# Router matmuls turned round, and three rounds of five expert places in the first expert loop

## The reference, cut to what matters

```python
def routed_moe(h2d, router_w, router_b, w_gate, w_up, w_down):
    aff = jax.nn.sigmoid(jnp.dot(h2d, router_w).astype(F32))      # tokens x 16
    ...  # best group of four experts, the best two experts in it, weights wts
    def expert_block(args):
        xblk, e = args
        hid = jax.nn.silu(xblk @ w_gate[e]) * (xblk @ w_up[e])    # 1024 -> 1024
        return hid @ w_down[e]
    ...
    out = jnp.zeros((n_tok + 1, d_), F32).at[row_tok].add(yb * row_w[:, None])
```

## Time and profile before

| | us |
|---|---|
| median of 3 runs (2302.38 to 2303.32) | 2302.49 |
| the profiled execution, its own time | 2303.21 |
| its span in the trace | 2301.4 |
| PE busy in the span | 2105.7 (91%) |
| layer 0, end of the shift to first expert matmul | 524.6 to 562.5 |
| layer 0, expert places | 562.5 to 1090.9 |
| layer 1, end of the shift to first expert matmul | 1307.2 to 1329.9 |

### The profile page before, as it was taken

One profiled execution on the slowest core, in us unless ns is written; L12 is line 12 of the kernel. 1 busy time (PEld: TensorE's weight loads), 2 busy tenths in 40 slices (PEclk: granted clock), 3 DMA queues, 4 the chain that ended last, 5 costly groups with the idle time before them and its releaser, 6 DMA issues.

```text
span 2301.4 us, 26458 instructions
## 1 busy us (share of the span) xinstructions
PE 2105.7 (91%) x10534; PEld 1152.9 (50%) x10534; DVE 692.6 (30%) x1682; ACT 403.2 (18%) x862; POOL 48.0 (2%) x64
## 2 busy tenths in 40 slices
PE   5999999897999999999499799999999899998997
PEld 2345447745333333444275733333333676577886
DVE  2045118524111111110438311111111588711411
ACT  2014210012111111000216211111111332421101
POOL 0000000001000000000100000000000000000000
PEclk8999999996999999999699899999999899798998
DMA  9661229111999999998330279999999633232240
GB/s 361 234 220 37 73 89 389 51 69 57 400 427 429 427 428 427 428 427 312 132 110 2 98 330 428 429 428 428 428 429 422 237 109 100 94 127 102 80 140 19
DMA packets 114049, 572.94 MB, mean 249 GB/s; under 512 B 6080, under 2 KB 20672, under 8 KB 89264
## 3 DMA queue, kind: packets, MB, share of 16 engines
q1 hardware_dynamic: 105568, 545.57, 59.2%
q0 software_dynamic: 5648, 20.47, 2.4%
q10 hardware_dynamic: 2752, 5.77, 0.6%
HBM read 562.87 MB, written 8.91 MB: 248 GB/s over the span
## 4 chain that ended last, share of the span: by engine, by line
PE 77%; DMA 13%; DVE 6%; ACT 2%; issue 2%; SPq 1%; PEld 0%; POOL 0%; ACTq 0%; DVEq 0%; PEldq 0%; POOLq 0%
PE banks L494 25%; DMA weight_ring<-in_moe_w_down 7%; PE banks L925 6%; PE banks L876 6%; PE banks L1024 4%; PE banks L910 4%; PE banks L508 3%; DMA weight_ring<-in_moe_w_up 3%; PE banks L706 2%; PE banks L979 2%; PE banks L892 2%; PE banks L1011 2%; PE banks L686 2%; PE banks L537 2%; DVE pages L1789 1%
## 5 line engine op out<-in xcount | busy, mean ns | idle before, releaser
L494 PE MATMUL banks<-pages,weight_ring 128*128 128x256 f32 (+1 forms) x2240 | 578.9, 419 | 11.2 <-DVEq L2312 3.4
L494 PEld LDWEIGHTS banks<-pages,weight_ring 128*128 128x128 f32 x2240 | 428.9, 193 | 160.1 <-issue 106.5
L925 PE MATMUL banks<-weight_ring,pages 128*64 128x512 f32 x1024 | 228.5, 597 | 5.9 <-DMA weight_ring<-in_moe_w_up 5.9
L1581 ACT ACTIVATE pages<-banks 128x512 f32<-128x512 f32 (+1 forms) x149 | 82.2, 572 | 676.3 <-PE banks L1024 129.0
L1472 ACT ACTIVATE pages<-banks 128x256 f32<-128x256 f32 (+2 forms) x214 | 92.0, 452 | 603.8 <-PE banks L494 426.5
L876 PE MATMUL banks<-weight_ring,pages 128*64 128x512 f32 x832 | 185.6, 601 | 8.5 <-DMA weight_ring<-in_moe_w_up 3.8
L1789 DVE TENSOR_TENSOR pages<-banks,pages 128x512 f32<-128x512 f32 (+3 forms) x157 | 90.3, 616 | 294.4 <-PE banks L1037 147.4
L1789 DVE TENSOR_TENSOR pages<-pages 128x512 f32<-128x512 f32 (+9 forms) x271 | 163.6, 628 | 8.3 <-DVE pages L1789 2.5
L1789 DVE TENSOR_TENSOR pages<-pages,banks 128x512 f32<-128x512 f32 (+1 forms) x41 | 28.2, 687 | 455.2 <-PE banks L925 219.8
L925 PEld LDWEIGHTS banks<-weight_ring,pages 128*64 128x64 f32 x1024 | 71.4, 137 | 157.9 <-issue 141.4
L1024 PE MATMUL banks<-weight_ring,pages 128*64 128x512 f32 x512 | 114.9, 597 | 13.1 <-DVE pages L2214 12.5
(11 more groups left out here) (281 smaller groups left out, 1877.4 us busy)
## 6 DMA issues: line engine op xcount, KB each, us to landing
weight_ring<-in_moe_w_gate SPq DMA_DIRECT2D x64, 2048.0 KB, 17.9
weight_ring<-in_moe_w_up SPq DMA_DIRECT2D x64, 2048.0 KB, 21.1
weight_ring<-in_moe_w_down SPq DMA_DIRECT2D x64, 2048.0 KB, 20.5
weight_ring<-in_ada_w SPq DMA_DIRECT2D x24, 2048.0 KB, 16.2
weight_ring<-in_even_w_in SPq DMA_DIRECT2D x18, 2048.0 KB, 19.8
weight_ring<-in_odd_w_in SPq DMA_DIRECT2D x8, 2048.0 KB, 8.8
weight_ring<-in_odd_w_out SPq DMA_DIRECT2D x6, 2048.0 KB, 8.1
weight_ring<-in_odd_w_qkv SPq DMA_DIRECT2D x3, 2048.0 KB, 10.6
```

What stands on the lines that cost most here:

```text
L494: last = pe.matmul(b[:, 0:w], s[:, k, m * P:(m + 1) * P], src(k)[:, t0:t0 + w], start=(k == 0), stop=(k == nk - 1))
L925: last = pe.matmul(b[64 * a:64 * a + 64], xg[:, par, k, 64 * half:64 * half + 64], w_[:, k, 512 * a:512 * a + 512], start=(half == 0 and k ...
L1581: act.activation(dst, banks_mem[:, use(l, job)[0], 0:n], func).then_inc(moe_taken(l, job, 0)[0], 1)
```

## The change

Router: the stationary side is now the 16 router columns of a channel block and the 16 columns behind them (32 in all), on the column group `k % 4`; the moving side is `H[:, k]` with all tokens (512 or 256). Each of the 8 matmuls waits only for its own block of `H`. Four partial sums, 32 rows each, come out in `router_part`, which ACT copies to `pages`; a matmul with `fold` as the moving side for each tile of tokens adds the four and gives tokens x 16 as before. It stands behind the first 8 transposes.

First expert loop: the order of the places is now middle, narrow, middle, narrow, wide, three times, and a narrow one. There are as many of each kind as before. The loop holds five places and runs three times. `par` and `1 - par` are replaced by the table `BUFFER`; a wide place and the middle place behind it both use buffer 0. The layer 1 loop is what it was.

```diff
-KINDS = [MIDDLE, NARROW] * 6 + [WIDE, NARROW, WIDE, WIDE]
+FIVE = [MIDDLE, NARROW, MIDDLE, NARROW, WIDE]
+KINDS = FIVE * 3 + [NARROW]
...
+    router_part = pages(8, 512)
...
+    BUFFER = (0, 1, 0, 1, 0, 0)
...
-            pe.wait_ge(sem("norm_h"), norm_before(f"norm_e{l}") + KT * (nt // 2))
-            job = ("router", l)
+            job = ("router_part", l)
             b = open_job(job)
-            rw = vec("router_w").rearrange("p (k e) -> p k e", k=KT)
-            for t in range(nt):
-                for k in range(KT):
-                    last = pe.matmul(b[:, t * 16:(t + 1) * 16], H[:, k, t * P:(t + 1) * P], rw[:, k],
-                                     start=(k == 0), stop=(k == KT - 1))
+            at = VEC["router_w"][0]
+            for k in range(KT):
+                j = k % 4
+                pe.wait_ge(sem("norm_h"), norm_before(f"norm_e{l}") + (k + 1) * (nt // 2))
+                last = pe.matmul(b[32 * j:32 * j + 32, 0:w], small[:, at + 16 * k:at + 16 * k + 32], H[:, k, 0:w],
+                                 start=(k < 4), stop=(k >= 4), tile_position=(0, 32 * j))
             close_job(job, last)
...
+                if t == 0:
+                    wait_taken(pe, ("router_part", l))
+                    job = ("router", l)
+                    b = open_job(job)
+                    for t2 in range(nt):
+                        last = pe.matmul(b[:, 16 * t2:16 * t2 + 16], router_part[:, t2 * P:(t2 + 1) * P],
+                                         S("fold", 0, 16), start=True, stop=True)
                     close_job(job, last)
...
-                with pe.Fori(0, LOOPED[l], 2) as e:
-                    expert(p, e, 0, KINDS[0])
-                    expert(p, e + 1, 1, KINDS[1])
-                for e in range(LOOPED[l], N_EXP):
-                    expert(p, e, e % 2, KINDS[e])
+                if l == 0:
+                    with pe.Fori(0, 3) as i:
+                        for c in range(5):
+                            expert(p, i * 5 + c, BUFFER[c], FIVE[c], BUFFER[c + 1])
+                    expert(p, 15, BUFFER[5], NARROW, BUFFER[0])
+                else:
+                    with pe.Fori(0, N_EXP, 2) as e:
+                        expert(p, e, 0, NARROW, 1)
+                        expert(p, e + 1, 1, NARROW, 0)
...
             shift(f"norm_e{l}", l, 1, w)
+            evac(("router_part", l), router_part[:, 0:w], w)
             b = result(act, ("router", l))
...
-                gather(g + 1, 1 - par)
+                gather(g + 1, then)
```

More of the change, by code:

```diff
@@ L773, in experts @@
                         last = pe.transpose(b[:, k * P:(k + 1) * P], H[:, 4 * half + k, t * P:(t + 1) * P], ident)
+                    close_job(job, last)
+                if t == 0:
[5 more added lines that the diff above has]
+                                         S("fold", 0, 16), start=True, stop=True)
                     close_job(job, last)
@@ L848, in gather, with expert @@
                     turn_picked(g)
-            def expert(p, e, par, kind):
+            def expert(p, e, par, kind, then):
                 it = g = p * N_EXP + e
@@ L1590, in gather, with expert @@
                     take("spread", g, spread[:, par].rearrange("p n m -> p (n m)"), n=2 * P)
-            def expert(p, e, par, kind, rows_out=None):
+            def expert(p, e, par, kind, then, rows_out=None):
                 it = g = p * N_EXP + e
@@ L1644, in experts @@
             with act.Fori(0, np_) as p:
[L1645 to L1650, removed]
+                if l == 0:
+                    with act.Fori(0, 3) as i:
+                        for c in range(5):
+                            row = i * FIVE_ROWS + sum(FIVE[:c])
+                            expert(p, i * 5 + c, BUFFER[c], FIVE[c], BUFFER[c + 1], y_dram[bass.ds(row, FIVE[c])])
+                    expert(p, 15, BUFFER[5], NARROW, BUFFER[0], y_dram[ROWS_AT[15]:ROWS_AT[15] + NARROW])
+                else:
+                    with act.Fori(0, N_EXP, 2) as e:
+                        expert(p, e, 0, NARROW, 1)
+                        expert(p, e + 1, 1, NARROW, 0)
                 if l == 0:
@@ L2179, in add_rest, with expert @@
                 tt(y_rest[:, 512:1024], rest[32:64], hid[32:64, 1], ALU.add).then_inc(moe_taken(0, "dn1", 0)[0], 1)
-            def expert(p, e, par, kind, after=None):
+            def expert(p, e, kind, rest=None):
                 it = g = p * N_EXP + e
@@ L2190, in expert @@
                 select_slots(g + 1, col)
-                if l == 0 and after == MIDDLE:
-                    add_rest(it - 1, p * KINDS.count(MIDDLE) + e // 2 + 1)
+                if rest is not None:
+                    add_rest(it - 1, rest)
                 if l == 0:
@@ L2236, in experts @@
                     dve.sem_inc(sem("rows_known"), 1)
[L2237 to L2241, removed]
+                if l == 0:
+                    with dve.Fori(0, 3) as i:
+                        for c in range(5):
+                            expert(p, i * 5 + c, FIVE[c], 6 * p + 2 * i + (c + 1) // 2 if c in (1, 3) else None)
+                    expert(p, 15, NARROW)
+                else:
+                    with dve.Fori(0, N_EXP, 2) as e:
+                        expert(p, e, NARROW)
+                        expert(p, e + 1, NARROW)
                 if l == 0:
```

3 lines of the change are left out of this document (1 added, 2 removed).

## The result

The changed kernel takes 2285.24 us in the median of 4 runs (2278.15 to 2287.58), the kernel before, beside it, 2302.90. The ratio is 0.9917, with a 95% interval of 0.9895 to 0.9940: faster by 0.8%. The forecast was 2283.5, in a range of 2279 to 2290.5. The profiled execution took 2287.58 and has a span of 2285.5, 15.9 less than before.

The account below looks back on a forecast made before the run. PE bounds the kernel, through router work everybody awaits and waits for weights in layer 0's expert places. Terms 8.6 - 1.5 + 9.0 + 3.5 - 0.7 = 18.9 us gave a median of 2283.5, range 2279 to 2290.5.

Parts of the forecast that it names:

- The router in layer 0: Layer 0, end of ACT's shift to sigmoid: sigmoid at 529.85 instead of 538.50, 8.6 us earlier, at the lower clock.
- the end named for that case: Layer 0 router at full clock: transposes and fold halve, ACT's table load is late next, gain 10.8 us.
- The clock behind it: Layer 0 ranking up to 1.8 us slower, first middle place up to 2.4 more; 1.5 us charged of 0 to 4.2.
- Layer 1: Layer 1 router: sigmoid at 1310.8 instead of 1314.31, 3.5 us gained, less 0.7 charged for the clock.
- the 9.0 of starving: Layer 0 expert places: PE's time lost to late weight chunks, 9.0 us, all regained by the new order.
- The state behind a wide place: Layer 0 expert loop: weight ring full again after each wide place (PE 44.3 us, transfers 31.5), so later rounds don't starve.
- The end of the places: Behind layer 0's last place: smaller store against about 5 us of queued transfers; put at 0, between gain 2.3 and loss 3.
- the first rival: Layer 0 expert loop fetched again, two turns at 3 to 5 us plus clock dips: 6 to 10 us lost; 7%.
- the full price of 12 us: Second rival: loop fetch costs 12 us at each turn plus 2.4 of lower clock, 28.8 us, giving 2312; 4%.
- The starving didn't move: Third rival, layer 0 places: transfers don't catch up under the wide place; at most half of 9.0 gained, 2288 to 2292.5; 9%.
- the ends of the forecast: Whole kernel: 2279 with 10.8 in router, no clock price, smaller store; 2288 with 7.5 in places, full clock price, half the queue.
- The fourth rival: Routers of both layers: something else ends last, so their 10.9 us are lost, giving 2294.4; 4%.

Follow-up runs that it names:

- the experiment with the wide place last: Changed kernel with the odd_w_out chunks held until the y_rows gathers landed, plus the third wide place moved from place 14 to the end: 2277.67 us.
- the loop of eight: Changed kernel with the layer 1 expert loop made eight places a turn instead of two: 2286.40 us, in a single run.

## Why the prediction was right, point by point

- **The median** was forecast at 2283.5 and came out at 2285.24; the gain was 17.7 us by the medians and 15.9 in the profiles, for 18.9.
- **The router in layer 0**: 8.6 us forecast to the sigmoid, 10.9 measured. The step that failed is the clock of the stretch: I had left PE at the lower one, and its work under the shift brought back the full one from 523.6. It is the end named for that case, 10.8. ACT's copy and table load were then late next, as written there.
- **The clock behind it**: the ranking took 1.9 us more, just beyond what was allowed (1.8), while the first place, charged with up to 2.4 more, took 0.7 less. To the first place the gain is 37.94 - 29.08 = 8.9 us. With the 0.7 in the first place it is 9.6, for the 7.1 forecast with both charges.
- **Layer 1**: 4.3 to the sigmoid for 3.5, and 3.3 to the first expert matmul for 2.8. Where the clock rose to the full level, the rest followed the same steps.
- **The places**: 9.5 us in the profile of both changes together, 0.7 of it from the clock. That leaves 8.7 (9.46 - 0.74) for the 9.0 of starving; no wait for weights is left. The state behind a wide place is as it was reckoned, and the experiment with the wide place last starved by 5.1 us where the same arithmetic said 6.
- **The end of the places**: this is the term that was wrong. It was put at 0, between -3 and +2.3, and cost 4.4 us, beyond its end. The step that failed is "about 5 us of transfers are still queued": the queue was seen, but its price was taken from the store alone, and not from the eight gathers behind it, in front of which three chunks of 2 MB were issued. The store gained more than the 2.3 allowed, 4.0 us, but up to DVE's first sum the gathers lost 3.3 and in its wait for the second pair 4.1; the other 1.0 lies in small pieces. The 29.35 us of the kernel before already held 7.5 us of delay by the same chunks.
- **The sum was right in part since two misses cancel**: 2.5 more in layer 0's router and 0.5 in layer 1's, 4.4 less at the end; another 1.2 in the profile lie ahead of the router (0.85) and in the rest (0.4), where no work was changed.
- **The rivals**: in the changed kernel the fetch at the turns did not occur, shown by the absent queue and the gapless start of the place behind each turn. That was partly luck: with the old router in front the same loop was fetched, and then the price was about 1.0 us in late gathers, not the 3 to 5 us a turn of the first rival. That products in flight cover the halt, which was its counter-argument, fits, but is argued. In the loop of eight, with 2.0 us of products still to run, it was 4.88 us and 2.6 for the dip of the clock; the full price of 12 us was too high for either. The starving didn't move. The router's gain wasn't lost. The Trainium skill (Runtime: NRT & Kernel Launch, Instruction fetch mechanics) gives PE room for 2048 instructions, in blocks of 256. By that number the round of 1,638 should stay and the turn of 2,088 shouldn't; the second is what the trace shows, the first only eight profiles of ten. Its window of two blocks agrees with none of the loops that were kept, 2.7 blocks in the kernel before and 6.4 in the changed one.
- **Sums that don't come out**: the ends of the forecast, 2279 and 2288, follow from the terms named with them only without the smaller store and the queued transfers; with them they are 2277 and 2290. All of the gain is gone from a fetch of 7.1 us a turn on (2 x 7.1 and 2 x 2.4 of clock), not from 11.8. The fourth rival's 10.9 should be 12.1, or 9.9 with the charges for the clock. None of this touches the median.

## What to carry to other kernels

Where PE and the transfers are nearly even, look at the order of unequal pieces, not only at their sum: a long piece must come before the advance of the transfers is used up, and the deficits, added piece by piece, say where that is. Then ask what the queue of transfers holds at the end of the loop, because a small store and the gathers behind it share it with chunks that nobody needs yet; holding those for some 20 us was worth 10.3 us here, where the reordering saved 9.5 in the places. The waits of 3.6 and 5.1 us ahead of the ranking, a chain of small matmuls, cost twice, once themselves and once by the clock behind them. And look at the instruction queue of every version, not only of the one that was forecast: an edit elsewhere can change whether a loop is fetched anew.

## What the runs showed of the hardware

- Work of PE on 32-column groups, spread over 6.5 us, brought the full clock back; 3.6 us of idling lost it for the ranking, and idle matmuls in the same gap kept it for most of the ranking (6.16 us became 3.77).
- A loop of 1,638 records of PE was kept at its turns in eight profiles; in two, with 48 to 83 more records of PE ahead of it, it moved 18 and 19 packets of 16 KB between 700 and 1040 and PE did not halt. A loop of 2,088 moved ten packets in its second turn and halted PE for 4.88 us under full transfers.
- With the transfers full (391 to 415 GB/s) a store of 256 KB and the start of the first gather lie 6.9 us apart, and 4.2 us with 217 GB/s beside them; the next step, from that gather to its first use, took 10.1 us and 6.3. For the store of 512 KB it was 10.9 us with 268 GB/s and 3.6 with 209, so it is the chunks issued ahead that tell, more than the rate.
